# First norm of a decoder trunk in two halves of its features: order of the conditioning, and half of the first up tile between its steps

## What is computed

```python
c_act = jax.nn.silu(c)
for l in range(DEPTH):
    mod = (c_act @ P['ada_w'][l] + P['ada_b'][l]).reshape(B, 1, 3 * N_SUB, D_MODEL)

    def pre(y, j):
        return _rmsnorm(y, P['norm_g'][l, j]) * (1 + mod[:, :, 3 * j + 1]) + mod[:, :, 3 * j]

    x = x + 0.5 * mod[:, :, 2] * _swiglu(pre(x, 0), P['ffn_wg'][l, 0], P['ffn_wu'][l, 0], P['ffn_wd'][l, 0])
    h = pre(x, 1)
    ...
    x = x + mod[:, :, 5] * (merged @ P['w_out'][l])
    x = x + 0.5 * mod[:, :, 8] * _swiglu(pre(x, 2), P['ffn_wg'][l, 1], P['ffn_wu'][l, 1], P['ffn_wd'][l, 1])
```

## Time and profile before

| | us |
|---|---|
| median of three runs | 2518.48 |
| lowest and highest | 2517.38, 2518.59 |
| profiled execution, whole | 2517.25 |
| profiled execution, span | 2514.8 |
| PE busy in the span | 2465.9 |
| DVE, ACT, POOL busy | 1640.3, 1046.4, 1008.7 |

### The profile page before, as it was taken

The page is one execution under the profiler, slowest core; times in us unless marked ns, Lnnn a source line. Parts: engine busy times, 40 slices in busy tenths (PEclk is TensorE's granted clock), DMA queues, the critical chain, the costliest instruction groups (busy, mean ns, idle before and its releaser), DMA issues. The chain is left out here.

```text
span 2514.8 us, 59172 instructions
## 1 busy us (share of the span) xinstructions
PE 2465.9 (98%) x23812; PEld 2338.1 (93%) x23812; DVE 1640.3 (65%) x3406; ACT 1046.4 (42%) x1986; POOL 1008.7 (40%) x768
## 2 busy tenths in 40 slices
PE   6999999999999999999999999999999999999999
PEld 4999998999988999999999999989998899899999
DVE  5677683377884466858666858635778824859493
ACT  3434343333465343434443434443344643435252
POOL 3443445333313444444444444443342235344443
PEclk9999999999999999999999999999999999999999
DMA  7353526322213424423532433552232135122232
GB/s 273 122 181 119 174 101 217 145 69 93 98 60 109 167 96 135 163 98 109 188 116 89 179 118 135 185 216 69 69 104 69 60 118 185 68 94 100 94 108 93
DMA packets 112645, 313.56 MB, mean 125 GB/s; under 512 B 19132, under 2 KB 45802, under 8 KB 95226
## 3 DMA queue, kind: packets, MB, share of 16 engines
q1 hardware_dynamic: 103424, 290.60, 33.5%
q10 hardware_dynamic: 8970, 19.44, 2.1%
HBM read 299.56 MB, written 10.66 MB: 123 GB/s over the span
## 5 line engine op out<-in xcount | busy, mean ns | idle before, releaser
L1090 POOL TENSOR_TENSOR w_lo<-raw,w_hi 128x512 fp32r<-128x512 f32 (+1 forms) x440 | 551.1, 1278 | 904.3 <-ACT w_hi L1221 875.8
L1097 POOL TENSOR_TENSOR w_lo<-raw,w_hi 128x512 fp32r<-128x512 f32 x228 | 331.0, 1466 | 447.0 <-ACT w_hi L1258 447.0
L2706 PE MATMUL bank<-h_hi,w_hi 128*128 128x260 f32 (+1 forms) x1312 | 380.7, 290 | 4.1 <-POOL w_lo L1109 3.5
L1221 ACT CAST w_hi<-raw 128x1024 fp32r<-128x1024 f32 (+2 forms) x164 | 216.5, 1320 | 384.9 <-PE bank L2708 271.6
L2707 PE MATMUL bank<-h_hi,w_lo 128*128 128x260 f32 (+1 forms) x1312 | 369.6, 282 | 0.0
L2708 PE MATMUL bank<-h_lo,w_hi 128*128 128x260 f32 (+1 forms) x1312 | 369.3, 281 | 0.0
L2853 PE MATMUL bank<-t_hi,w_hi 128*128 128x260 f32 x1216 | 345.7, 284 | 7.5 <-DVE u L2156 4.5
L2707 PE MATMUL bank<-mid_hi,w_lo 128*128 128x260 f32 x1232 | 348.6, 283 | 0.0
L2706 PE MATMUL bank<-mid_hi,w_hi 128*128 128x260 f32 x1232 | 348.6, 283 | 0.0
L2708 PE MATMUL bank<-mid_lo,w_hi 128*128 128x260 f32 x1232 | 347.3, 282 | 0.0
L2855 PE MATMUL bank<-t_hi,w_lo 128*128 128x260 f32 x1216 | 343.9, 283 | 0.0
(11 more groups left out here) (398 smaller groups left out, 6241.9 us busy)
## 6 DMA issues: line engine op xcount, KB each, us to landing
raw<-in_w SPq DMA_DIRECT2D x120, 1024.0 KB, 4.9
raw<-in_w SPq DMA_DIRECT2D x128, 512.0 KB, 4.1
ada_ring<-in_ada SPq DMA_DIRECT2D x68, 256.0 KB, 5.5
ada_ring<-in_ada SPq DMA_DIRECT2D x48, 320.0 KB, 5.3
raw<-in_w SPq DMA_DIRECT2D x32, 384.0 KB, 3.2
ada_ring<-in_ada SPq DMA_DIRECT2D x48, 192.0 KB, 5.2
ada_low<-in_ada SPq DMA_DIRECT2D x20, 256.0 KB, 4.8
out_y<-x ACTq DMA_DIRECT2D x4, 1040.0 KB, 13.9
```

The source lines that it names most:

```text
L1090: last = pool.tensor_tensor(w_lo[j][:, cols], raw[j][:, cols], w_hi[j][:, cols].bitcast(F32), ALU.subtract)
L1097: pool.tensor_tensor(place(w_lo, l, stage, slot, piece), src, place(w_hi, l, stage, slot, piece).bitcast(F32), ALU.subtract).then_inc(sema ...
L1221: s.copy(w_hi[j][:, 0:n], raw[j][:, 0:n]).then_inc(head_split[j], 1)
L2706: mm(out, wh(wb), xh(xb), start=(n == 0), stop=False)
```

## The change

- The first norm is treated in two halves of the features. The pieces of ada parts are cut anew: part 0 now holds shift and scale of feature tiles 0 to 3 and part 1 those of tiles 4 to 7. For parts 0 and 1 of every group of three this makes four pieces to a step where there were two, of 128 to 384 columns; the bytes are the same. SP's program grows from 696 to 820 rows by it.
- SP loads weight slot 0 right behind x, then ada steps 0 to 15, then slot 1.
- The squares are added on DVE, not on POOL; the statistics follow ada step 4 instead of 9. ACT casts slot 0 ahead of the statistics' root.
- DVE works off tiles 0 to 3 (`first_half(0)`) after part 0, and tiles 4 to 7 after part 1. PE takes feature tiles 0 to 3 of the first up tile between ada steps 11 to 15 (`ADA_MEET`), then turns part 1, runs the 17 identity matmuls and takes tiles 4 to 7.
- POOL waits with slot 1's low parts until the low part of tile 6 is made.
- The gate half of slot 2 is cast in slot 0 instead of slot 1, in every FFN's first up stage.
- The identity matmuls of sub-layers 2 and 5 are gone.

```diff
-ADA_PIECES = (((0, 0, 640), (1, 0, 384)), ((0, 640, 512), (1, 384, 512)), ((0, 1152, 384), (1, 896, 640)))
-ADA_RUNS = (((0, 0, 3), (3, 6, 2), (5, 3, 3)), ((0, 8, 1), (1, 12, 3), (4, 9, 3), (7, 15, 1)),
+ADA_PIECES = (((0, 0, 384), (0, 640, 128), (1, 0, 128), (1, 384, 384)),
+              ((1, 128, 256), (0, 384, 256), (0, 768, 384), (1, 768, 128)),
+              ((0, 1152, 384), (1, 896, 640)))
+ADA_RUNS = (((0, 0, 3), (3, 8, 1), (4, 3, 1), (5, 9, 3)), ((0, 4, 2), (2, 6, 2), (4, 12, 3), (7, 15, 1)),
...
-ADA_STAT = 10
+ADA_STAT = 5
+ADA_MEET = {11: 0, 12: 1, 13: 2, 15: 3}
...
-BUSY = {0: 17, 2: 8, 5: 3}
+BUSY = {0: 17}
...
     for l in range(DEPTH):
+        keys += [(l, "norm", 0, n) for n in (0, 1)]
         keys += [(l, "ada", 1)] if l == 0 else []
-        keys += [(l, "norm", 0, n) for n in (0, 1)]
...
+        def tiles_ready(sub, k):
+
+            return 9 * sub + k + (2 if sub > 0 or k >= KT // 2 else 1)
...
-            for n in range(10):
-                load_ada(n)
-
...
             load_w(0, "up00", 0, 0)
-            for n in range(10, ADA_FIRST):
+            for n in range(ADA_FIRST):
                 load_ada(n)
             load_w(0, "up00", 0, 1)
...
-            for k in range(1, KT - 1):
-                add_square(0, k)
+            up_split(0, "up00", 0)
+            pool.wait_ge(h_lo_ready, tiles_ready(0, KT - 2))
+            up_split(0, "up00", 1)
...
                     if stage[:2] == "up":
-                        for slot in range(2 if stage[3] == "0" and (l, stage) != (0, "up00") else 0, slots):
+                        for slot in range(2 if stage[3] == "0" else 0, slots):
                             up_split(l, stage, slot)
...
                         high(0)
                         high(1)
+                        cast(l, stage, 2, SUM_1)
                         t_head(l, f, 1)
                     elif start and slot == 1:
                         silu(0)
                         silu(1)
                         t_head(l, f, 2)
-                        cast(l, stage, 2, SUM_1)
                         high(0)
                         cast(l, stage, 2, SUM_4)
                         high(1)
...
+            def first_norm():
+
+                for k in range(KT - 1):
+                    square(0, k)
+                last_square(0)
+                cast(0, "up00", 0, SUM_1)
+                cast(0, "up00", 0, SUM_4)
+                act.wait_ge(lb_exp, 1)
+                s.activation(lb_tmp[:, 0:2, :], lb_tmp[:, 0:2, :], ACT.Exp).then_inc(lb_exp, 1)
+                s.activation(sqrt_warm[:], ones[:, 0:1], ACT.Abs_reciprocal_sqrt)
+                roots(0)
+                for k in range(KT):
+                    if k % (KT // 2) == 0:
+                        tiles = slice(k, k + KT // 2)
+                        act.wait_ge(scaled_ready, k + 1)
+                        last = s.copy(h_hi[:, tiles, SEQ:COLS], h_s[:, tiles, :])
+                        if k > 0:
+                            last.then_inc(h_hi_ready, 1)
+                    act.wait_ge(scaled_ready, tiles_ready(0, k))
+                    s.copy(h_hi[:, k, 0:SEQ], scaled[:, k, :]).then_inc(h_hi_ready, 1)
...
+                        at = pair_cols(0, "up00", 1).start + i % 2 * PIECE
+                        last = s.copy(w_hi[i // 2][:, at:at + PIECE], raw[1][:, i * PIECE:(i + 1) * PIECE])
+                        if i % 2 == 1:
+                            last.then_inc(head_split[1] if i == 3 else piece_cast, 1)
...
+            v.memset(bank[5][:], 0.0).then_inc(ada_taken0, 1)
+
+            for k in range(1, KT - 1):
+                dve.wait_ge(tile_squared, k + 1)
+                if k > 1:
+                    dve.wait_ge(squares_added, k - 1)
+                v.tensor_tensor(sq_sum[:], sq_sum[:], sq[k % 2][:], ALU.add).then_inc(squares_added, 1)
...
+            statistics(0)
             ada_rows(0)
+            unit_tile(0)
+            unit_tile(1)
             ada_take(0)
-            statistics(0)
-            for k in range(UNIT_TILES - 1):
+            unit_tile(2)
+            unit_tile(3)
+            first_half(0)
+            for k in range(4, KT - 1):
                 unit_tile(k)
             ada_rows(1)
-            unit_tile(UNIT_TILES - 1)
+            unit_tile(KT - 1)
+            rstd, done = wait_side(dve, 0, "norm", 0, 0)
+            v.tensor_copy(sqrt_warm[:], rstd[:, 0:1]).then_inc(done, 1)
             ada_take(1)
+            first_half(1)
...
+            def open_first(l, stage):
+
+                wait_gate(l, stage, 0)
+                wait_up(l, stage, 0)
+                for b in range(4):
+                    take_main(b, main_use(l, stage))
+
+            def first_tile(l, stage, sub, k):
+
+                (gh, gl), (uh, ul) = direct_weights(l, stage, 0)
+                (x0h, x0l), (x1h, x1l) = moving(h_hi, h_lo, 0), moving(h_hi, h_lo, 1)
+                wait_h(sub, k)
+                split_products([gate_bank(0), gate_bank(1), up_bank(0), up_bank(1)], [k] * 4,
+                               [(gh(k), gl(k))] * 2 + [(uh(k), ul(k))] * 2,
+                               [(x0h(k), x0l(k)), (x1h(k), x1l(k))] * 2)
...
+                    if sub > 0:
+                        open_first(l, stage)
+                    if sub == 0:
+                        pe.wait_ge(ada_taken, 1)
                     for _ in range(BUSY.get(sub, 0)):
-                        mm(bank[3][:, 0:P], ident[:], ident[:], start=True, stop=True)
+                        mm(ada_bank[:, 0:P], ident[:], ident[:], start=True, stop=True)
+                    for k in range(KT // 2 if sub == 0 else 0, KT):
+                        first_tile(l, stage, sub, k)
...
-                if n == KT - 1:
+                if n == ADA_STAT - 1:
                     pe.wait_ge(const_loaded, 16 * 12)
                     pe.wait_ge(setup_done, 4)
+                    statistics(0)
+                if n in ADA_MEET:
+                    if ADA_MEET[n] == 0:
+                        open_first(0, "up00")
+                    first_tile(0, "up00", 0, ADA_MEET[n])
                 if n % KT == KT - 1:
                     ada_turn(n // KT)
-                if n == ADA_STAT - 1:
-
-                    statistics(0)
```

More of the change, by code:

```diff
@@ L1425, in norm @@
                 if sub == 0:
-                    for k in range(KT - 1):
-                        square(0, k)
-                    s.activation(sqrt_warm[:], ones[:, 0:1], ACT.Abs_reciprocal_sqrt)
-                    last_square(0)
-                for n, cols in ((0, slice(0, SEQ)), (1, slice(SEQ, COLS))):
-                    src, _ = wait_side(act, l, "norm", j3, n)
-                    s.activation(root[:, cols], src[:, 0:cols.stop - cols.start], ACT.Abs_reciprocal_sqrt,
-                                 scale=1.0 / D_MODEL, bias=eps[:]).then_inc(root_ready, 1)
-                if sub == 0:
-                    cast(0, "up00", 0, SUM_1)
-                    cast(0, "up00", 0, SUM_4)
-                elif j3 == 1:
+                    first_norm()
+                    return
+                roots(sub)
+                if j3 == 1:
                     head_after(l, f"down0{LAST}", KT - 1)
@@ L1937, in norm @@
                 link(v.tensor_tensor(h_s[:], x[:, :, SEQ:COLS], md[:, 8:16, 1:CC], ALU.mult))
-                if sub > 0:
-                    statistics(sub)
+                statistics(sub)
                 rstd, done = wait_side(dve, l, "norm", j3, 0)
@@ L2655, in merge, with first_half, scale, low @@
                 dve.wait_ge(x_restored, 32 * (l + 1))
+            def first_half(part):
+                md, tiles, gains = mod[0], slice(4 * part, 4 * part + 4), slice(8 + 4 * part, 12 + 4 * part)
+                rstd, _ = wait_side(dve, 0, "norm", 0, 0)
+                rstd_s, done_s = wait_side(dve, 0, "norm", 0, 1)
+                def scale(k):
+                    v.tensor_scalar(scaled[:, k, :], scaled[:, k, :], md[:, 8 + k, 0:1], md[:, k, 0:1],
+                                    ALU.mult, ALU.add).then_inc(scaled_ready, 1)
+                def low(k):
+                    if k == 4 * part:
+                        dve.wait_ge(h_hi_ready, k + 1)
+                        dve.wait_ge(scaled_ready, k + 1)
+                        last = v.tensor_tensor(h_lo[:, tiles, SEQ:COLS], h_s[:, tiles, :],
+                                               h_hi[:, tiles, SEQ:COLS].bitcast(F32), ALU.subtract)
+                        if part == 1:
+                            last.then_inc(h_lo_ready, 1)
+                    dve.wait_ge(h_hi_ready, tiles_ready(0, k))
+                    dve.wait_ge(scaled_ready, tiles_ready(0, k))
+                    v.tensor_tensor(h_lo[:, k, 0:SEQ], scaled[:, k, :], h_hi[:, k, 0:SEQ].bitcast(F32),
+                                    ALU.subtract).then_inc(h_lo_ready, 1)
+                link(v.scalar_tensor_tensor(out=md[:, gains, :], in0=md[:, gains, :], scalar=1.0,
```

(18 more changed lines are left out.)

58 lines of the change are left out of this document (17 added, 41 removed).

## The result

| | before | changed |
|---|---|---|
| median of 12 runs, us | 2518.81 | 2524.15 |
| lowest and highest, us | 2517.38, 2522.38 | 2521.00, 2526.39 |
| profiled execution, us | 2517.25 | 2524.64 |

The ratio is 1.002 with a 95% interval from 1.0012 to 1.0028. The forecast of 2518.0 missed, and 2524.15 lies just above the range that ended at 2523. The time is that of rival (b), 2524, which had a chance of 0.10.

What follows compares the result with a forecast made beforehand. PE, busy 2465.9 of 2514.8 us, was taken as the bound. From 2517.25, 0.5 gained at the start and 0 for the other three terms gave 2516.75; with 1.23 added, 2518.0 us, range 2513 to 2523.

Steps and rivals of the forecast that it cites:

- rival (b): SP becomes the limit and is slower, at the start or with late weight loads in three stages: 2524 or 2533; chance 0.10.
- Finer ada pieces later on: I take 0: Stages with densest ada loads: SP near its limit, but 2 us of slack; 0, bound 1 to 3 us in each of three.
- ada 15 after 41.7: Start: sign deciding for SP as the limit, the last of the first 16 ada steps landing later than 41.7 us.
- the 0.1 us a step taken for finer pieces: First ada steps at the start: the finer pieces move the same bytes and delay each step by 0.1 us.
- The start, "0.5 us gained": Startup in the new order: first tile 2.0 us earlier, mostly taken back by slot 3; 0.5 gained, between 3.2 gained and 2 lost.
- prod: Product of gate and up half in slot 1, on DVE: at 57.9 us, 3.8 us after the first tile instead of 0.1.
- the wait in slot 2: Start, middle of slot 2: PE waits 1.9 us for the up half, ready at 73.3 and wanted at 71.4.
- DVE's loss: Start, POOL's low parts of slot 1: DVE loses about 1.0 us to each POOL operation beside it.
- ada 15's end: Start, last ada step ahead of the first tile's second half: ends at 42.3 us, bounds 39.5 to 44.
- rival (c): Clock low for longer, in tiles 0 to 2 or the two second FFNs: 1.7 to 5 us lost, about 2521; chance 0.09.
- The cast: Slot 2's gate half cast one slot earlier: wait moves to mid-slot 2; 0 per later FFN, bounds 1.55 gained, 0.6 lost.
- The identity matmuls: Eight and three left out in the two second FFNs: h_lo sets the start, so 0; 1.7 us each if the clock falls.

Runs made afterwards that it cites:

- two pieces again: Changed kernel with the old two pieces to a step from ada step 16 on, four kept in the first 16: 2519.5 us, ratio 1.0005.
- finer later pieces alone: Kernel before with four pieces to an ada step from step 16 on, nothing else changed: 2523.93 us, ratio 1.0022.
- the burst spread: Changed kernel with ada steps 28 to 31 loaded one behind each of slots 4 to 7 of the first down stage: 2521.33 us, ratio 1.001.
- the idle stretches filled: Changed kernel, two pieces from step 16 on, plus 8 identity matmuls ahead of part 0's turn and 12 ahead of tile 0: 2519.11 us, ratio 1.0007.

## Why the prediction was wrong

**The step that failed is "Finer ada pieces later on: I take 0".** Its working was right in kind (SP issues a piece in 0.46 us, weights stand behind it) and looked at the wrong place, the stages with most ada loads; there the changed kernel indeed lost little (about 1 us near 1640, tenths near 400). At the end of the first down stage eight issues in a row became sixteen, ahead of the loads with which DVE begins the next up stage: 3.3 us lost, about half of it because the weights were issued later and half because they took longer to land, for which the prediction had no term. With two pieces again 1.1 us were left of 5.3, finer later pieces alone cost 6.0, and with the burst spread 3.4 were left. The bound, 1 to 3 us in each of three stages, was of the right size, and rival (b) held it with its 2524, at a chance of 0.10. That the time came out at (b)'s figure is in part luck: one stage lost more than (b) gave it, the others less, and the start lost by the clock.

Rival (b) at the start (ada 15 after 41.7) did not come about: ada 14 and 15 ran in one go at 44.09 without waiting. But the 0.1 us a step taken for finer pieces was too little: 41.02 - 36.06 = 5.0 us for 16 steps in the old order, 0.3 each. In the new order the slower tiles covered it.

The Trainium skill, "DMA: Bandwidth & Descriptors", section "🔬 Bandwidth", asks for large transfers, and the change that went against it lost by it. The traces agree in kind: from 140 to 144 us 260 and 248 GB/s moved with the smaller pieces, where 402 and 419 had moved before. The price that the runs show is 0.47 us of SP for every DMA, and weights late behind them.

**The start, "0.5 us gained", was 2.1 lost.** Most terms of the chain held: the statistics' start at 22.3 (22.1), prod 3.5 us behind the first tile (3.8), the wait in slot 2 2.06 us (1.9), DVE's loss 1.07 us for each POOL operation (1.0). Mis-sized was ada 15's end, 45.1 instead of 42.3. 1.15 us of this are tile 0's later start, and nearly all of that is the second half of the statistics, 2.28 us where the sum had the earlier trace rows's 1.24. It is a matter of the execution: it took 1.29 to 2.28 us in eight traces with the new start and 1.23 to 2.15 in six with the old one, while the granted clock in the rows was 1.00. The lower clock made tile 0 longer by 1.0, the ada step by 0.4 and tile 1, 1.88 instead of 1.44, by 0.4. That was rival (c), at the lower end of its price, and it came together with (b) rather than instead of it. The prediction also took the start of one execution for the rule; in others the kernel before loses to the clock there too. With the idle stretches filled the clock stayed up and the first tile ended 1.1 us sooner than with two pieces alone, from -0.6 to -1.7.

**The cast: right**, 0 in the later FFNs; the wait moved by half a slot and became 1.8 us. **The identity matmuls: right in sum**, 0, and for a reason that the prediction didn't have: the clock did fall, for 1.5 us, and the wait for POOL behind it became shorter by as much.

**Open.** Why the weights took 7.17 us to land instead of 5.31 isn't shown; with eight larger pieces the time varied from 5.3 to 7.6. Of 5.3 us between medians and 7.4 us between the two profiled executions the difference is of the kind that comes and goes.

## What to carry to other kernels

Where one queue issues everything, count DMAs and not bytes alone: look for the longest row of issues ahead of a load that an engine will soon wait for, wherever that is in the program, and ask both when that load is issued and how long it then takes to land. A table shared by all stages carries a local cut into all of them. Before a forecast rests on one execution's row, see whether other executions of the same kernel have it. An engine that loses time ahead of a wait doesn't lose it twice: look for the wait that ends last before removing what comes earlier. And work that is put between small steps of the matmul engine needs that engine kept busy ahead of it; here it began at the lower clock otherwise.

## What the runs showed of the hardware

- SP's issue took 0.47 to 0.48 us for a piece of 64 KB and for one of 320 KB alike (7.54 us for 16, 3.87 for 8), and 0.47 to 0.58 in the start under load.
- A load of weights was in use 5.31 us after its issue in the kernel before, 7.17 us after it behind sixteen small pieces, and 5.3 to 7.6 us in runs with eight larger ones.
- Behind PE idle stretches of 1.8 to 2.4 us the granted clock stood at 0.50 (1.2 GHz) for about 3 us, and the stretch of matmuls lost about 1.5 us; it happened in some executions and not in others at the same place (in the kernel before without identity matmuls: a wait of 2.41 us at 914.28 without a fall, and one at 2152.48 with 0.50 from 2154 to 2156).
- A DVE subtraction of 32 elements to a partition took 1.28 us beside POOL (56.52) and the like 0.18 without (60.00): it lost 1.1 us, as much as the ones of 1008 elements beside it (2.29 and 2.35 against 1.20). POOL paid too: its four subtractions took 6.47 us beside these, and 4.96 at 31.65 in the kernel before.
